# Attention phase of a hybrid sparse decoder layer: top-k mask pieces, search ends, transposes by product, constants' loads

## The reference

```python
# group A (letter D in the kernel): 8 heads of 64, shared keys, top-256 keys of a learned index
logits = jnp.einsum('bqhd,bsd->bqhs', iqb, ik)                       # 8 index heads of 32
index = jnp.einsum('bqh,bqhs->bqs', iwb, jax.nn.relu(logits)) * idx_scale
_, sel = lax.top_k(jnp.where(causal[None], index, -jnp.inf), topk)
# ... attention over the chosen keys

# group B: 8 heads in 2 groups; three branches, weighted by sigmoid gates
p_c = masked_softmax(s_c, ...)   # C: 127 compressed keys
imp = jnp.einsum('bgrqc,cj->bgqj', p_c, overlap)    # -> importance of 32 blocks of 64 keys
_, sel = lax.top_k(imp, 8)       # S: attention over the 8 chosen blocks
# W: sliding window of 512 keys
return gb[..., 0:1] * o_c + gb[..., 1:2] * o_s + gb[..., 2:3] * o_w
```

## Time and profile before

| | us |
|---|---|
| three timed runs | 4032.27, 4021.42, 4033.93 (median 4032.27) |
| the profiled execution | 4017.63 |
| its span, first to last instruction | 4015.8 |

### The profile page before, as it was taken

The page is one execution under the profiler, slowest core; times in us unless marked ns, Lnnn a source line. Parts: engine busy times, 40 slices in busy tenths (PEclk is TensorE's granted clock), DMA queues, the critical chain, the costliest instruction groups (busy, mean ns, idle before and its releaser), DMA issues. The chain is left out here.

```text
span 4015.8 us, 56010 instructions
## 1 busy us (share of the span) xinstructions
PE 3672.0 (91%) x19448; PEld 3108.9 (77%) x19448; DVE 1852.0 (46%) x4296; ACT 1655.0 (41%) x2690; POOL 777.6 (19%) x1650
## 2 busy tenths in 40 slices
PE   6999768997999999999899797999999999999997
PEld 5999646786787887877678586788788788878885
DVE  4222135656666677667665253333343243324323
ACT  2000025656677766778783332322233222223221
POOL 0000023444434233332331132000020020002001
PEclk9999768988899999999999898999999999999998
DMA  4221220000000000000000354333333433433342
GB/s 137 77 72 61 67 52 20 23 21 15 16 16 16 8 16 16 15 7 5 9 6 6 115 159 149 104 98 127 97 99 102 142 100 96 143 106 95 97 138 74
DMA packets 302064, 273.15 MB, mean 68 GB/s; under 512 B 32544, under 2 KB 249760, under 8 KB 299680
## 3 DMA queue, kind: packets, MB, share of 16 engines
q1 hardware_dynamic: 300368, 268.31, 21.6%
q10 hardware_dynamic: 1488, 2.20, 0.2%
HBM read 218.57 MB, written 51.90 MB: 67 GB/s over the span
## 5 line engine op out<-in xcount | busy, mean ns | idle before, releaser
L2261 DVE TENSOR_TENSOR f_w_lo<-f_raw,f_w_hi 128x1024 fp32r<-128x1024 f32 x264 | 337.4, 1279 | 883.5 <-ACT f_w_hi L2213 883.5
L2213 ACT ACTIVATE f_w_hi<-f_raw 128x1024 fp32r<-128x1024 f32 x264 | 279.9, 1060 | 882.4 <-PE f_acc L2165 336.9
L1319 ACT ACTIVATE a_p_t<-a_ps_st 128x512 f32<-128x512 f32 x716 | 437.3, 614 | 373.2 <-PE a_ps_st L1209 198.4
L1326 ACT ACTIVATE a_junk_a<-a_index,a_tk 128x512 fp8e4<-128x512 f32 (+13 forms) x336 | 445.4, 1326 | 100.7 <-DVE a_halves L1436 50.3
L1235 PEld LDWEIGHTS a_ps_o<-a_vsl,a_p_t 128*128 128x128 f32 x2176 | 319.9, 211 | 22.0
L2165 PE MATMUL f_gate<-f_x_hi,f_w_hi 128*128 128x512 f32 x704 | 275.0, 391 | 30.1 <-DVE f_w_lo L2261 30.1
L1235 PE MATMUL a_ps_o<-a_vsl,a_p_t 128*128 128x65 f32 x2176 | 302.5, 287 | 0.0
L1235 PEld LDWEIGHTS a_ps_o<-a_dv,a_p_t 128*128 128x128 f32 x2176 | 292.5, 195 | 9.9
L2165 PE MATMUL f_acc<-f_w_hi,f_g_hi 128*128 128x512 f32 x704 | 278.4, 395 | 17.3 <-DVE f_y L2317 12.6
L2146 POOL TENSOR_TENSOR f_rstd<-f_aggr,f_eps 128x1 f32<-128x1 f32 x16 | 6.5, 406 | 1402.1 <-DVE f_aggr L2291 1402.1
L2165 PE MATMUL f_acc<-f_w_lo,f_g_hi 128*128 128x512 f32 x704 | 277.3, 394 | 0.0
(11 more groups left out here) (268 smaller groups left out, 7560.8 us busy)
## 6 DMA issues: line engine op xcount, KB each, us to landing
f_raw<-in_w_gate SPq DMA_DIRECT2D x88, 512.0 KB, 3.8
f_raw<-in_w_up SPq DMA_DIRECT2D x88, 512.0 KB, 3.9
f_raw<-in_w_down SPq DMA_DIRECT2D x88, 512.0 KB, 3.3
z_scratch<-p_z SPq DMA_DIRECT2D x16, 1120.0 KB, 5.2
pw_raw<-in_w_in SPq DMA_DIRECT2D x16, 560.0 KB, 3.7
px_raw<-in_x_t SPq DMA_DIRECT2D x16, 512.0 KB, 6.4
o_scratch<-a_oacc SPq DMA_DIRECT2D x32, 256.0 KB, 2.1
m_o_in<-o_scratch SPq DMA_DIRECT2D x16, 512.0 KB, 4.6
```

The source lines that it names most:

```text
L1319: act.activation(p_t[:, s % PT_RING, :], ps_st[s % ST_BANKS][:, :], ACT.Exp, scale=SCALE).then_inc(exp_done, 1)
L1326: act.activation(junk_a[:, 0:w], index[RANK[t] % 2][:, 0:w], ACT.Sign, bias=thr, scale=-1.0, accum_out=cnt, saturate=False).then_inc(count ...
L2213: act.activation(w_hi[:, slot], raw[:, parity], ACT.Copy).then_inc(hi_done, 1)
L2261: dve.tensor_tensor(w_lo[:, slot], raw[:, parity], w_hi[:, slot].bitcast(F32), ALU.subtract).then_inc(lo_done, 1)
```

## The change

Four things in the attention phase:

1. `topk_due` is one formula for all tiles, counted back from the tile's first `D` step; `end` is counted back from it by three steps a chunk, and `above`, `rank` and `pick` take a step each instead of overlapping.
2. The planner's costs of `prep` and `aug` are lower.
3. The transposes of `prep` and `aug` become float32r products with an identity `ident_r`; `a_naug` and `a_daug` become float32r.
4. `ident` moves to the staged constants; the staged load goes out before the first keys and has its own semaphore; the kept constants are loaded after the keys, and VectorE waits for them only before the first step. TensorE waits for `ident_r`.

```diff
-SIDE_COST = {"max": 727, "cmax": 600, "idx": 680, "prep": 450, "aug": 440}
+SIDE_COST = {"max": 727, "cmax": 600, "idx": 680, "prep": 300, "aug": 290}
...
-CONST = (("ident", P), ("keep", 62), ("add", 62), ("halve", NSTEP + 1),
-         ("win", W_TILES * P), ("cmp", 248), ("blk", N_SLC), ("one", 2), ("ovl", N_SLC))
+CONST = (("keep", 62), ("add", 62), ("halve", NSTEP + 1),
+         ("win", W_TILES * P), ("ident", P), ("cmp", 248), ("blk", N_SLC), ("one", 2), ("ovl", N_SLC))
...
     def topk_due(self, t):
-        if t >= TILES - LAG:
-            return self.first("D", t - 1, 1)
-        if t == TILES - 1 - LAG:
-            return self.first("S", TILES - 2, 1)
-        return self.first("S", t + LAG) if t < 5 else self.first("W", t + LAG) + 2
+        return self.first("D", t) - 3 * self.chunks[t] - 2
...
-            end = self.topk_due(t) - 2 * nch - 4
+            end = self.topk_due(t) - 3 * nch - 3
...
-                self.chores[end + 1 + c].append(("above", t, c))
-                self.chores[end + 2 + c].append(("rank", t, c))
-                self.chores[end + 3 + nch + c].append(("pick", t, c))
+                self.chores[end + 1 + 2 * c].append(("above", t, c))
+                self.chores[end + 2 + 2 * c].append(("rank", t, c))
+                self.chores[end + 2 + 2 * nch + c].append(("pick", t, c))
...
-            self.chores[end + 1 + nch].append(("room", t, 0))
+            self.chores[end + 2 * nch].append(("room", t, 0))
...
-                at = max(at, self.search[before][1] + 2 * self.chunks[before] + 4)
+                at = max(at, self.topk_due(before))
...
+        ident_r = sb("a_ident_r", [P, P], F32R)
...
-        aug_n = sb("a_naug", [P, 2, 8, P])
-        aug_d = sb("a_daug", [P, 8, P])
+        aug_n = sb("a_naug", [P, 2, 8, P], F32R)
+        aug_d = sb("a_daug", [P, 8, P], F32R)
...
             load_q("N", 0)
+            sp.dma_start(stage[:, 0:CONST_COLS - KEPT_COLS], consts[:, KEPT_COLS:CONST_COLS]).then_inc(stage_ld, 16)
+            load_k(0)
             sp.dma_start(cst[:, :], consts[:, 0:KEPT_COLS]).then_inc(const_ld, 16)
-            load_k(0)
-            sp.dma_start(stage[:, 0:CONST_COLS - KEPT_COLS], consts[:, KEPT_COLS:CONST_COLS]).then_inc(const_ld, 16)
...
-                    mm = pe.transpose(out[:, (b - b0) * P:(b - b0 + 1) * P], src.bitcast(F32), const("ident", 0, P))
+                    mm = pe.matmul(out[:, (b - b0) * P:(b - b0 + 1) * P], src, ident_r[:, :], start=(b == b0), stop=(b == b0 + nb - 1), skip_group_check=True)
...
-                    mm = pe.transpose(out[:, h * P:(h + 1) * P], aug_of(kind, i)[:, 4 * g + h, :], const("ident", 0, P))
+                    mm = pe.matmul(out[:, h * P:(h + 1) * P], aug_of(kind, i)[:, 4 * g + h, :], ident_r[:, :], start=(h == 0), stop=(h == 3), skip_group_check=True)
...
-            pe.wait_ge(const_ld, 32)
+            pe.wait_ge(ident_set, 1)
...
-            dve.wait_ge(const_ld, 32)
-            mine(dve.tensor_copy(ident_b[:, :], const("ident", 0, P)))
+            dve.wait_ge(stage_ld, 16)
+            dve.tensor_copy(ident_r[:, :], staged("ident")).then_inc(ident_set, 1)
+            mine(dve.tensor_copy(ident_b[:, :], staged("ident")))
...
+            dve.wait_ge(const_ld, 16)
             held = []
```

More of the change, by code:

```diff
@@ L799, in attention_phase @@
         const_ld = sem("a_const_ld")
+        stage_ld = sem("a_stage_ld")
         zk_ld = sem("a_zk_ld")
@@ L807, in attention_phase @@
         rows_set = sem("a_rows_set")
+        ident_set = sem("a_ident_set")
         split_done = {k: sem(f"a_split{k}") for k in "KIND"}
@@ L1066, in block_mask @@
                 pool.tensor_copy(mask_s[:, g, t * P:(t + 1) * P], diag_b()).then_inc(mask_s_done, 1)
-            pool.memset(aug_n[:, :, :, :], 0.0).then_inc(aug_clear, 1)
-            pool.memset(aug_d[:, :, :], 0.0).then_inc(aug_clear, 1)
+            pool.memset(aug_n[:, :, :, :].bitcast(F32), 0.0).then_inc(aug_clear, 1)
+            pool.memset(aug_d[:, :, :].bitcast(F32), 0.0).then_inc(aug_clear, 1)
             prep_q("N", 0)
```

## The result

Both kernels ran side by side six times: before 4020.4 us (median, 4008.9 to 4033.9), after **4063.9 us** (4050.7 to 4077.8). The ratio is 1.0106, with a 95% interval of 1.0074 to 1.0139: the change costs 43 us, where 31.5 us of gain was forecast. The profiled execution of the changed kernel has a span of 4066.1 us (before 4015.8), TensorE busy 3740.6 us (3672.0) and a mean clock of 0.933 (0.948).

What follows compares the result with a forecast made beforehand. Attention was taken as TensorE's, less 146 us idle and some time at half clock. Terms -40 - 16 + 18 + 8 - 1.5 = -31.5 us, carried to the 4032.3 us median, gave 4001 us; 8-in-10 range 3957 to 4045.

Steps and rivals of the forecast that it cites:

- The products: TensorE's 248 aug and prep groups: float32r products instead of transposes cost +0.06 us a group, taken as +8 us.
- clock rival: TensorE's clock: if transposes keep it from rising and products don't, -30 us more, 3971 us; chance 0.12.
- Search ends: Tiles 6 to 14: ends away from GpSimd's query split and pieces apart cut TensorE's waits and half speed, -40 us.
- tile 5: Tile 5's short search: 24 steps instead of 17 for its 24 counts cut idle and half speed, -16 us.
- stack: VectorE, tiles 5 to 12: picks now right before the C finishes make TensorE wait, +18 us.
- Constants: Start of the kernel: the constants' load ahead of the keys lets VectorE's tables start sooner, -1.5 us.
- Planner costs: Lower prep and aug costs: an aug step may take a second scan, same work, 0 us, bounds -5 and +8.
- The stalls only move: Rival: new search ends meet the index split, W's scans and C; -1.5 us in all, 4031 us; chance 0.22.

Runs made afterwards that it cites:

- e2_place: Kernel before with the placing alone changed (due step, search ends, pieces, start of index products): ratio 0.9972, -11 us.
- e5_noprod: Changed kernel with only the transposes back in place of the products: ratio 0.9994 to the kernel before, -2 us.
- e4_const: Kernel before with the constants' new order alone, transposes kept: ratio 0.9998, -1 us.
- e11_f32prod: As e3_prod, but with plain float32 identity products instead of float32r: ratio 1.0194 to the kernel before, +78 us.
- e3_prod: Kernel before with the float32r products and the constants' new order, old placing and planner costs: ratio 1.0132, +53 us.

## Why the prediction was wrong, by its own steps

- **The products** (+8 forecast, bounds -20 and +35): the mis-sized term, and the one that turned the forecast gain into a loss. Its working of a group was about right, 0.05 us for the 0.06 derived from the earlier trace rows, 12 us in all. The rest of the measured 45 to 54 is the clock, which the sum held constant for this term. The bounds covered only the group's own length.
- **The clock rival** had the sign wrong. It let the products give back 30 us; they took more. The Trainium skill, page "TensorE: Matmul & The Clock Gate", Part 4, says that a transpose doesn't count as busy the way a product does and full speed doesn't engage for it. For this mix, float32 transposes among products, the measurement decides against it: with transposes the phase has 236 us at half speed, with float32r products in their place 403. The prediction saw one sign, the 1.00 of the earlier trace rows with transposes in the stretch, and used it only to lower the chance, not to ask for the opposite case.
- **Search ends** (-40), **tile 5** (-16) and the **stack** (+18), together -38, measured -11. The step that failed is "with GpSimd's collision gone": it counted the distance to the query splits (and to the index split) and not to the accumulates, which GpSimd does in the same step ahead of `below`. The forecast's own test, VectorE's wait for `below` under 6 us, came out at 18.1. Four steps earlier it is 8.9, and the gain is then -36. With the accumulate behind `below` it is 8.7 and the gain -20, so this step explains 9 of the 27 us missed at the best estimate; the cause of the rest stays open.
- **Tile 5's search** went as forecast in waits: TensorE's longest one for `a_q` there is 1.7 us, not 5.7. Over the steps 120 to 160 `e2_place` is 11.6 us shorter than before, where 16 was forecast; that is all of its -11, so by the profiled executions the search ends and the stack together gave nothing.
- **The stack** before `C`'s finishes: the idle time at the finishes near the due steps of tiles 7 to 12 was 17 to 18 us before. With the placing alone (`e2_place`) it is 19, so little of the 14 forecast shows; with the lower costs besides it is 25 to 26 (`e5_noprod`), and about 24 in the changed kernel, 4 us a tile, the limit that the forecast named.
- **Constants** (-1.5): right for the first transposes, and next to nothing at the end (`e4_const` -1 us, -5 to +3). SP's first query load to TensorE's first transposes took 6.75 us before (525.27 to 532.02) and takes 5.26 after (530.10 to 535.36), 1.5 less. But the first score came 20.0 us behind that load and comes 19.6: it waits for the first aug's rows, not for the transposes.
- **Planner costs** (0, bounds -5 and +8): +28 in the old plan, clear of the bounds, and +9, +13 and -14 in the three others, where the intervals reach into them. "The work is the same" was no reason for zero where TensorE's stalls come from which scan meets which piece.
- **"The stalls only move"** came nearest for the placing: ends -10, tile 5 -8, stack +10, so -8, where `e2_place` measured -11. The sum is in part luck, since tile 5 gave all of it. The rival missed what the forecast missed, the products' clock.

## What to carry to other kernels

Changing the kind of work that the tensor engine does can change the clock that it is granted, in either direction: measure the clock of an isolated variant before a swap of transposes for products is priced by its length alone. When pieces are moved in an in-order engine's program, list everything that stands in the same step ahead of them, the small accumulates as well as the big splits, and follow who waits behind. And in a kernel with several stalling engines a plan's parameter has no price of its own: the same edit measured +28 us in one plan and +9 in another, and moving it the other way cost 14. Such a term deserves a range of tens of microseconds, not a narrow one about zero.

## Not expected of the hardware

- Some 960 float32 transposes by TensorE, replaced by as many float32r products, raised the time at half speed from 236 to 403 us of a phase of 1700, with as many falls of the clock (27 and 25) that last twice as long; replaced by float32 products (two passes each) they lowered it to 205. One float32r product more beside the transposes of each group left it where one transpose more does (258 and 257).
- Clock and idle time went opposite ways: with `e11_f32prod`, `e3_prod` idles least of the old plans (123 us each), and it has the lowest clock of all (0.926 over the run). The link that the prediction rested on, half speed follows idle time, holds only while the kind of work stays the same.
